# Three seven-product steps instead of two in each gate-up unit, and one low-part instruction a step

## The reference, cut to what matters

```python
D_MODEL = 2048
D_FF = 5632
def swiglu(hn, w_gate, w_up, w_down):
    return (jax.nn.silu(hn @ w_gate) * (hn @ w_up)) @ w_down
```

## Time and profile before

| | |
|---|---|
| time, median of 3 runs | 2617.34 us (2615.75 to 2618.74) |
| the profiled execution | 2618.52 us, its span from first to last instruction 2616.7 us |
| TensorE busy | 2575.2 us (98% of the span), 11985 matmuls |
| VectorE busy | 1784.8 us (68%) |
| ScalarE busy | 1332.1 us (51%) |
| mean granted clock of TensorE | 0.998 of full speed |
| moved by DMA | 477.93 MB, 183 GB/s on average |

### The profile page before, as it was taken

One profiled execution on the slowest core, in us unless ns is written; L12 is line 12 of the kernel. 1 busy time (PEld: TensorE's weight loads), 2 busy tenths in 40 slices (PEclk: granted clock), 3 DMA queues, 4 the chain that ended last, 5 costly groups with the idle time before them and its releaser, 6 DMA issues.

```text
span 2616.7 us, 30595 instructions
## 1 busy us (share of the span) xinstructions
PE 2575.2 (98%) x11985; PEld 2130.4 (81%) x11985; DVE 1784.8 (68%) x2027; ACT 1332.1 (51%) x1823; POOL 232.2 (9%) x290
## 2 busy tenths in 40 slices
PE   9999989999999999999999999999999999999998
PEld 7888867888888888888788888888888888888876
DVE  6876756785787578765556686687568765565656
ACT  6453345574475347544455564476447654434432
POOL 1000010200000000040033300000000033130000
PEclk9999999999999999999999999999999999999999
DMA  7552225655565566556555655665556555556664
GB/s 226 180 166 89 81 89 152 204 183 193 193 209 177 196 206 203 181 201 220 177 169 193 209 194 185 201 194 193 193 193 209 179 198 165 177 177 182 179 237 152
DMA packets 251440, 477.93 MB, mean 183 GB/s; under 512 B 19336, under 2 KB 23168, under 8 KB 250656
## 3 DMA queue, kind: packets, MB, share of 16 engines
q1 hardware_dynamic: 246064, 467.92, 55.4%
q10 hardware_dynamic: 4656, 7.15, 0.8%
q0 software_dynamic: 576, 0.90, 0.2%
HBM read 473.82 MB, written 2.10 MB: 182 GB/s over the span
## 4 chain that ended last, share of the span: by engine, by line
PE 90%; DVE 6%; issue 1%; ACT 1%; ACTq 0%; DMA 0%; SPq 0%; POOL 0%; DVEq 0%
PE ps L1266 18%; PE ps L1268 18%; PE ps L1267 18%; PE ps L1279 10%; PE ps L1281 10%; PE ps L1280 10%; DVE w_lo L1874 1%; PE ps L1027 1%; PE ps L1386 1%; DVE gs L1546 1%; PE ps L1372 1%; ACT w_hi L867 0%; ACT e_s L1009 0%; DVE we_lo L1939 0%; DVE w_lo L1933 0%
## 5 line engine op out<-in xcount | busy, mean ns | idle before, releaser
L1874 DVE TENSOR_TENSOR w_lo<-raw,w_hi 128x1024 fp32r<-128x1024 f32 (+1 forms) x568 | 700.9, 1251 | 368.2 <-ACT w_hi L867 363.0
L867 ACT CAST w_hi<-raw 128x1024 fp32r<-128x1024 f32 (+1 forms) x568 | 580.9, 1045 | 451.6 <-PE ps L1268 379.2
L1266 PE MATMUL ps<-w_hi,xh 128*128 128x512 f32 (+1 forms) x1184 | 470.6, 397 | 5.6 <-DVE w_lo L1874 5.0
L1933 DVE TENSOR_TENSOR w_lo<-raw,w_hi 128x1024 fp32r<-128x1024 f32 x320 | 382.9, 1218 | 131.8 <-ACT w_hi L893 131.5
L893 ACT CAST w_hi<-raw 128x1024 fp32r<-128x1024 f32 x320 | 334.0, 1053 | 264.2 <-PE ps L1281 195.1
L1268 PE MATMUL ps<-w_hi,xl 128*128 128x512 f32 (+1 forms) x1184 | 459.3, 388 | 0.0
L1267 PE MATMUL ps<-w_lo,xh 128*128 128x512 f32 (+1 forms) x1184 | 458.5, 387 | 0.0
L1266 PE MATMUL ps<-w_hi,fh 128*128 128x512 f32 x1056 | 415.0, 393 | 4.0 <-DVE w_lo L1874 4.0
L1268 PE MATMUL ps<-w_hi,fl 128*128 128x512 f32 x1056 | 411.5, 390 | 0.0
L1267 PE MATMUL ps<-w_lo,fh 128*128 128x512 f32 x1056 | 411.3, 389 | 0.0
L1279 PE MATMUL ps<-w_hi,xh 128*128 128x512 f32 x1040 | 404.7, 389 | 0.0
(11 more groups left out here) (353 smaller groups left out, 2337.2 us busy)
## 6 DMA issues: line engine op xcount, KB each, us to landing
raw<-in_ffn_w_gate SPq DMA_DIRECT2D x176, 512.0 KB, 3.8
raw<-in_ffn_w_up SPq DMA_DIRECT2D x176, 512.0 KB, 4.7
raw<-in_ffn_w_down SPq DMA_DIRECT2D x176, 512.0 KB, 4.3
raw<-in_w_in SPq DMA_DIRECT2D x112, 512.0 KB, 3.8
raw<-in_even_w_in SPq DMA_DIRECT2D x80, 512.0 KB, 3.7
raw<-in_odd_w_in SPq DMA_DIRECT2D x64, 512.0 KB, 4.5
raw<-in_odd_w_out SPq DMA_DIRECT2D x32, 512.0 KB, 4.5
raw<-in_w_out SPq DMA_DIRECT2D x32, 512.0 KB, 4.2
```

The costliest lines, as they stand in the source:

```text
L867: act.copy(w_pair(w_hi, w2_hi, blk, k), raw[:, slot, 0:2, 0:blk.width]).then_inc(hi_ready, 1)
L1266: pe.matmul(acc(blk, t), hi_x[:, blk.lk0 + k, tok], hi_w, start=(k == 0), stop=False)
L1874: TT(w_pair(w_lo, w2_lo, blk, k), raw[:, slot, 0:2, 0:w], w_pair(w_hi, w2_hi, blk, k).bitcast(F32), ALU.subtract).then_inc(lo_ready, 1)
L1933: TT(w_lo[:, at:at + 2, :], raw_pair(step, c), w_hi[:, at:at + 2, :].bitcast(F32), ALU.subtract).then_inc(sw_lo, 1)
```

## The change

A unit has three seven-product steps: (0, 2, 4), in an entry unit (2, 4, 6). The step at which the M banks are done, and with it `combine` and the copy of M1, stays at step 5, or 7 in an entry unit. The two subtractions of a step become one over all four tiles (`raw_step`), in plain and seven-product steps alike. It waits for both copies of ScalarE. `c_out` 3 comes behind it in step 1. TensorE waits once for the four tiles of a step, and in a seven-product step once more for `we_lo`. The semaphore `sw_lo` is counted anew (`l0`, `lows`), and the sums wait for `we_lo` of the seven-product step before. Everything else is as it was: the loads, the copies of ScalarE, the order of the units.

```diff
-        self.sevens = (2, 6) if entry else (0, 4)
+        self.sevens = (2, 4, 6) if entry else (0, 2, 4)
...
+                step.g0, step.mm0, step.l0 = groups, mms, lows
+                lows += 1 + step.seven
...
+                    step.n7, step.sums_free = n_seven, sums_free
+                    sums_free = lows
...
-                raw_user[2 * step.d] = raw_user[2 * step.d + 1] = ("sw_lo", groups)
+                raw_user[2 * step.d] = raw_user[2 * step.d + 1] = ("sw_lo", lows)
...
+        def raw_step(step):
+
+            both = raw2 if step.d == 2 else raw[:, 2 * step.d:2 * step.d + 2]
+            return both.rearrange("p c k n -> p (c k) n")
...
-                    if step.i == sb.sevens[1] + 1:
+                    if step.i == sb.sevens[-1] + 1:
...
-                        pe.wait_ge(sw_lo, step.g0 + 1)
+                        pe.wait_ge(sw_lo, step.l0 + 1)
                         three(M1, x_parts(k, 0), w_hi[:, 0, :], w_lo[:, 0, :], first, final)
-                        pe.wait_ge(sw_lo, step.g0 + 2)
                         three(M5, s_parts(step, 0), w_hi[:, 2, :], w_lo[:, 2, :], first, final)
-                        pe.wait_ge(sw_lo, step.g0 + 3)
+                        pe.wait_ge(sw_lo, step.l0 + 2)
                         three(M7, s_parts(step, 2), we_hi[:, 0, :], we_lo[:, 0, :], first, final)
...
+                    pe.wait_ge(sw_lo, step.l0 + 1)
                     for c, banks in enumerate(((C11, C21), (C12, C22))):
-                        pe.wait_ge(sw_lo, step.g0 + c + 1)
                         for t in range(NT):
...
                 dve.wait_ge(s_raw[step.d], 32 * (step.uses + 1))
+                if step.sums_free:
+                    dve.wait_ge(sw_lo, step.sums_free)
...
-                    for c in range(2):
-                        dve.wait_ge(sw_hi, step.g0 + c + 1)
-                        at = step.at + 2 * c
-                        TT(w_lo[:, at:at + 2, :], raw_pair(step, c), w_hi[:, at:at + 2, :].bitcast(F32),
-                           ALU.subtract).then_inc(sw_lo, 1)
-                        if c == 0 and step.i == 1 and after_super:
-                            c_out(p, 3)
+                    dve.wait_ge(sw_hi, step.g0 + 2)
+                    at = slice(step.at, step.at + 4)
+                    TT(w_lo[:, at, :], raw_step(step), w_hi[:, at, :].bitcast(F32), ALU.subtract).then_inc(sw_lo, 1)
+                    if step.i == 1 and after_super:
+                        c_out(p, 3)
```

More of the change, by code:

```diff
@@ L190, in plan @@
     mix_t0 = mix_h0 = None
-    q = groups = mms = n_sb = n_seven = placed = 0
+    q = groups = lows = sums_free = mms = n_sb = n_seven = placed = 0
     raw_user = [None] * 6
@@ L201, in plan @@
                 step.q, step.d, step.uses = q, q % 3, q // 3
-                step.g0, step.mm0 = groups, mms
+                step.g0, step.mm0, step.l0 = groups, mms, lows
+                lows += 1 + step.seven
                 step.raw_waits = {u for u in raw_user[2 * step.d:2 * step.d + 2] if u}
@@ L209, in plan @@
                     step.ext_wait = ext_user
-                    step.n7 = n_seven
+                    step.n7, step.sums_free = n_seven, sums_free
+                    sums_free = lows
                     n_seven += 1
@@ L1289, in super_block @@
                     if step.seven:
-                        first, final = step.i == sb.sevens[0], step.i == sb.sevens[1]
+                        first, final = step.i == sb.sevens[0], step.i == sb.sevens[-1]
                         if first and after_super:
```

## The result

The changed kernel takes 2680.39 us (median of 4 runs, 2679.20 to 2681.95) against 2618.04 for the kernel before on the same chip. The ratio is 1.0234 (95% interval 1.0221 to 1.0247), so the change costs 62.4 us. Forecast were 2679.3 and +62. The profiled execution took 2681.03 us, 2680.5 were forecast.

What follows compares the result with a forecast made beforehand. TensorE, busy for 98% of the span, was taken as the bound, with VectorE's lateness making it wait. 31.2 + 19.2 + 1.4 + 11.2 - 2.7 = 60.3, with about 1.7 for slow first matmuls +62: 2679.3 us, range 2666 to 2692.

Steps and rivals of the forecast that it cites:

- The matmul's worth: TensorE: three matmuls fewer in each of 20 units at 0.227 us each, 0.68 us a unit, 13.6 us saved.
- The price of the merged instruction: VectorE's 2048-column subtraction: length 2.28 us, distance 2.20, saving 0.07 a step against two subtractions at 2.27.
- The unit: Unit following a plain one: 46.07 us instead of 42.16, 0.68 saved and 4.6 new waits; eight of them +31.2 us.
- The units behind an entry: Late VectorE makes TensorE wait 6.83 us instead of 1.35, less 0.68: +4.8 in four units, +5.6 in two.
- The waits in all: TensorE's waits for lines of VectorE grow by some 74 us in all.
- What was put at no cost: The sums' wait for the last we_lo and the weight loads: no time added.
- The loads: Tightest load, of step 7, there about 29.7, first read at 32.6: cover 2.9 us, gone with landings over 7.6.
- Count only: Rival: all new VectorE work hides, only the fewer matmuls count, 2603.7 us, faster by 13.6; chance 0.05.
- Part of the waits: Rival: ScalarE's placing copies let the copies of step 5 through, its wait goes in 16 units, 2653 us; chance 0.07.
- Clock: Rival: new waits up to 1.9 us drop TensorE's clock from 2.4 to 1.2 GHz, +33 us, 2712; chance 0.03.

Runs made afterwards that it cites:

- the last experiment: Against the kernel before: third seven-product step (entry units 2 and 4), low parts in halves, products reordered, placing copies and feature split later; 2605.06 us, ratio 0.9950.
- The third: Changed kernel with ScalarE's second eight placing copies moved from behind the copies of step 4 to behind those of step 5; 2653.09 us, 27.3 below the changed kernel.
- the fourth experiment: Changed kernel with the low parts of step 1 alone in two halves again; 2662.93 us, 17.5 less than the changed kernel.
- the tenth: Three seven-product steps (entry 2 and 4), low parts in halves, the four sums made by GpSimd instead of VectorE; 2656.99 us, ratio 1.0145 to the kernel before.
- the kernel with extra work in the late place: Changed kernel plus 2.48 us of needless VectorE work in 14 units, behind gate_super, ahead of the sums of step 2; 2721.35 us, ratio 1.0390 to the kernel before.

## Why the prediction was right, point by point

**The matmul's worth.** 60 matmuls fewer, 0.227 us each. The experiments don't measure this alone. What they show is that it can be had: in the last experiment a unit of 183 matmuls took 41.90 us with one short gap in it, and 183 x 0.227 is 41.5.

**The price of the merged instruction.** Its length is 2.28 us (mean 2285 ns) and its distance to the next 778.76 - 776.55 = 2.21; 2.20 had been taken from the earlier trace rows. The Trainium skill's fixed extra for each instruction ("VectorE: DVE Perf Modes", TRN2 errata) would have made it 2.11 and the total some 5 us less, 2674. For the length of single instructions the traces agree: 2 x 1218 ns (1024 columns, before) are 151 ns more than 2285. For the distance, which is what counts here, they do not: two such instructions back to back take 0.07 us more than a merged one, not 0.16.

**The unit.** The four new starts are right to 0.06 us, the period is 46.15 instead of 46.07. The chain was right too: silu, copy, merged low parts at step 1; `gate_super`, sums, merged low parts at step 2; placing copies, copies, merged low parts at step 5. The third and the fourth experiment cut it at two of these places and got the 27 and the 17.5 us.

**The units behind an entry.** 719.16 to 725.97 is 6.81 us from step 0 to step 1; the working had 4.76 + 0.31 + 1.87 = 6.94. In the first group the step-0 wait was to be 1.7 and is 1.52 + 0.16 = 1.68, with an idle time of 1.52 in the row of that place:

```profile
561.72 0.47 PE L1286 MATMUL ps<-w_hi,xh 128*128 128x512 f32 x1 [1.52 <-DVE w_lo L1940]
...
568.53 0.50 PE L1286 MATMUL ps<-w_hi,xh 128*128 128x512 f32 x1 [1.54 <-DVE w_lo L1940]
```

**The waits in all.** Forecast was a growth of some 74 us; it is 65.2, so this sign missed by 9 us. The total asks for 62.4 + 13.6 = 76.0, and the other 10.8 us are slower first matmuls: behind a gap 12 matmuls take 2.85 to 2.90 us where 12 x 0.227 is 2.72, and there are 85 gaps now where there were 12. The working put the matmuls behind a wait at full pace, so it counted nearly all of this as wait, and 1.7 us beside it. The sum is right all the same, and not by luck: where VectorE sets the time of the next step, a slower matmul only shortens the wait before it, as the prediction said.

**What was put at no cost.** The loads: no wait of TensorE for a DMA occurs in the units, and 2.5 us more of VectorE work did not bring one. ScalarE's copies wait for an up tile six times, as before (17.4 us in all, before 16.5). The 0.41 us in the prediction's sum for the loads stands in none of its rows; without it the cover is 3.3 us instead of 2.9, and nothing else changes. **The rivals.** Count only: wrong by 77 us. Part of the waits: this would have been 2653, and it is what the third experiment measured (2653.09) once the placing copies really let step 5 through; in the change they don't. Clock: granted 1.00 in all units, as forecast. The margin was small: in the kernel with the sums on GpSimd a gap of 1.79 us brought the lower clock, as told below, and the longest gap of the changed kernel is 1.55.

## What to carry to other kernels

When the producer works at 85% of a stretch and the consumer at 100%, don't ask whether the new work fits by load; write out when each piece is ready and when it is first read, with distances between starts as prices. A handful of rows gave that table here, and it foretold nine of ten other kernels within 5 us; the tenth failed because the durations themselves changed. Merging instructions that have separate producers and separate consumers saves their fixed part once (0.07 us) and makes the first consumer wait for the last producer (0.8 to 1.7 us before steps 0 and 1 with the merging alone), so merge only where both come together anyway. And look first at which large pieces meet on the feeding engine: here moving the entry units' second seven-product step from 6 to 4 brought 8.9 us with no work saved.

## What the runs showed of the hardware

**The clock behind gaps.** In the units of the kernel after, each of TensorE's gaps (idle for up to 1.55 us) is followed by 12 matmuls that take 2.85 to 3.18 us, those with a second short gap included, and the granted clock stays at 1.00. In the kernel with extra work in the late place the gap before step 2 is 3.67 us, and the clock falls at each of these 14 gaps. In the place shown the pitch goes from 0.23 to 0.43 us some 0.6 us after the start; in others the lower clock is there from the first matmul. Timeline of TensorE in that kernel, then two of its stretches (PEclk is the third number from the end):

```profile
787.50 0.50 PE L1286 MATMUL ps<-w_hi,xh 128*128 128x512 f32 x1 [3.67 <-DVE w_lo L1940]
787.84 0.41 PE L1287 MATMUL ps<-w_lo,xh 128*128 128x512 f32 x1
788.07 0.61 PE L1288 MATMUL ps<-w_hi,xl 128*128 128x512 f32 x1
788.47 0.63 PE L1286 MATMUL ps<-w_hi,s_hi_x 128*128 128x512 f32 x1
...
791.03 0.61 PE L1286 MATMUL ps<-we_hi,s_hi_x 128*128 128x512 f32 x1
791.46 0.41 PE L1287 MATMUL ps<-we_lo,s_hi_x 128*128 128x512 f32 x1
...
780.00:800.00 20.00, 16.33 (x65) 12.99 (x64) 18.91 (x17) 13.85 (x22) 0.00 (x0) 0.91 0.45 151
...
800.00:820.00 20.00, 19.54 (x87) 15.81 (x86) 15.92 (x14) 12.72 (x15) 0.00 (x0) 1.00 0.65 211
```

So the lower of the two levels (1.2 GHz) is in force from 788.07 to 791.46. The 12 matmuls behind such a gap take 4.2 to 5.3 us. In this place they take 4.43, which is 1.3 more than the 3.16 at the same step of the changed kernel. Later waits give it back: that before step 5 is down from 1.54 to 0.62, and that before M7 of step 4 is gone. In six of the 14 places the 12 matmuls take 5.29 us, and the waits can't give all of it back. Those six units are 0.5 to 0.8 us longer than the other eight of their kinds (49.4 to 49.6 us against 48.8, and behind an entry unit 50.5 to 50.8 against 50.0). That is 4.0 us in all, about what the time lies over the forecast.

The clock rival of the prediction was priced for gaps of up to 1.9 us. Gaps of 1.55 in the changed kernel did not bring the lower clock, nor did those of 1.72 in the kernel with step 1 in halves. In the kernel with the sums on GpSimd the two longest gaps in the units, 1.79 us each, did. Timeline of TensorE at the first of them:

```profile
697.15 0.50 PE L1286 MATMUL ps<-we_hi,s_hi_x 128*128 128x512 f32 x1 [1.79 <-DVE we_lo L1932]
...
698.39 0.63 PE L1287 MATMUL ps<-we_lo,s_hi_x 128*128 128x512 f32 x1
698.82 0.63 PE L1288 MATMUL ps<-we_hi,s_lo_x 128*128 128x512 f32 x1
```

So a kernel with waits only a little longer than those forecast here could have met that rival.

**VectorE and GpSimd.** Three GpSimd sums beside VectorE instructions, from the timelines of the kernel with the sums on GpSimd:

```profile
763.84 0.69 DVE L1908 TENSOR_TENSOR gs<-ps,hb 128x512 f32<-128x512 f32 x1
...
765.63 2.20 DVE L1926 TENSOR_TENSOR w_lo<-raw,w_hi 128x1024 fp32r<-128x1024 f32 x1
...
764.07 1.31 POOL L2189 TENSOR_TENSOR sums<-raw 128x512 f32<-128x512 f32 x1 [3.45 <-DVE we_lo L1932]
...
765.45 1.30 POOL L2191 TENSOR_TENSOR raw<-raw 128x512 f32<-128x512 f32 x1
766.70 2.29 POOL L2192 TENSOR_TENSOR sums<-sums,raw 128x512 f32<-128x512 f32 x1
```

Beside a VectorE instruction with one input in PSUM (`c_out`) a sum takes 1.31 us, and `c_out` keeps its 0.68. The low parts have both inputs in SBUF. They begin 0.18 us behind the second sum; that sum keeps its 1.30, and they take 2.20 instead of 1.22. The third sum begins while they are at work and takes 2.29. So in these rows the one that comes second is longer by about what is left of the first (1.0 us longer, with 1.1 left, both times). The Trainium skill has this rule ("SBUF — State Buffer", section Who interferes with whom): a VectorE instruction with two SBUF inputs contends with a GpSimd instruction that reads SBUF, one with at most one SBUF input doesn't, and the trace agrees. The size was not foreseen: VectorE is busy for 1833.8 us in this kernel, and for 1840.1 in the one with the same order and its own sums, so that the second engine relieved it of nearly nothing.
